# Expert results through DRAM instead of scatter products, and gate and up weights in pieces of 256 input rows

## The reference, cut to what matters

```python
def moe_swiglu(h, router, wg, wu, wd):
    logits = (h @ router).astype(jnp.float32)
    top_v, top_i = lax.top_k(logits, TOP_K)
    gates = jax.nn.softmax(top_v, axis=-1)
    out = jnp.zeros_like(h)
    for e in range(N_EXPERTS):
        gate_e = jnp.sum(jnp.where(top_i == e, gates, 0.0), axis=-1)[..., None].astype(h.dtype)
        out = out + gate_e * swiglu(h, wg[e], wu[e], wd[e])
    return out
...
x = x + moe_swiglu(rmsnorm(x, p['norm_ffn_odd'][i]), p['moe_router'][i], p['moe_w_gate'][i],
                   p['moe_w_up'][i], p['moe_w_down'][i])
y = rmsnorm(x, p['final_norm'])
```

## Time and profile before

| | us |
|---|---|
| median of 3 runs | 1320.86 (1320.65 to 1324.37) |
| the profiled execution | 1327.41 |
| its span in the profile | 1325.7 |
| TensorE busy | 1299.6 (98%) |
| VectorE busy | 373.8 (28%) |
| ScalarE busy | 169.9 (13%) |
| GpSimd busy | 61.0 (5%) |

### The profile page before, as it was taken

One profiled execution on the slowest core, in us unless ns is written; L12 is line 12 of the kernel. 1 busy time (PEld: TensorE's weight loads), 2 busy tenths in 40 slices (PEclk: granted clock), 3 DMA queues, 4 the chain that ended last, 5 costly groups with the idle time before them and its releaser, 6 DMA issues.

```text
span 1325.7 us, 17071 instructions
## 1 busy us (share of the span) xinstructions
PE 1299.6 (98%) x7217; PEld 826.4 (62%) x7217; DVE 373.8 (28%) x869; ACT 169.9 (13%) x367; POOL 61.0 (5%) x87
## 2 busy tenths in 40 slices
PE   8999999999999999999999999999999999999997
PEld 6878788888888888867843433434334444444452
DVE  5537775421111113984400110011100110110101
ACT  2241423010000100013200000000000000101002
POOL 1013110000000201100000000000000000000000
PEclk8999999999999999999799999999999999999999
DMA  8639633565456424354699999999999999899994
GB/s 289 206 130 304 221 96 96 191 179 168 127 166 223 143 72 127 132 198 197 267 388 424 408 424 425 408 424 410 424 425 424 424 406 425 323 359 418 409 423 188
DMA packets 105484, 380.81 MB, mean 287 GB/s; under 512 B 7580, under 2 KB 62796, under 8 KB 80778
## 3 DMA queue, kind: packets, MB, share of 16 engines
q1 hardware_dynamic: 97811, 359.46, 69.9%
q0 software_dynamic: 3216, 11.54, 2.7%
q10 hardware_dynamic: 4386, 8.76, 2.1%
HBM read 371.96 MB, written 8.86 MB: 287 GB/s over the span
## 4 chain that ended last, share of the span: by engine, by line
PE 89%; DVE 7%; ACT 1%; DMA 1%; SPq 1%; issue 1%; DVEq 0%; ACTq 0%
PE ps L1746 30%; PE ps L2278 21%; PE ps L2317 13%; PE ps L2264 6%; PE ps L2272 3%; DVE both L1450 3%; PE ps L1999 3%; PE ps L2328 2%; PE ps L2299 1%; PE ps L1991 1%; PE ps L1977 1%; PE ps L2211 1%; PE ps L2148 1%; PE ps L2200 1%; DMA both<-in_w_in_even_dram 1%
## 5 line engine op out<-in xcount | busy, mean ns | idle before, releaser
L1746 PE MATMUL ps<-both 128*128 128x264 f32 x2080 | 474.3, 390 | 0.5 <-DMA both<-in_w_in_even_dram 0.3
L1746 PEld LDWEIGHTS ps<-both 128*128 128x128 f32 x2080 | 397.0, 192 | 72.3 <-issue 2.7
L2278 PE MATMUL ps<-both 128*64 128x384 f32 (+1 forms) x1792 | 280.9, 466 | 0.8 <-ACT both L1050 0.8
L2278 PEld LDWEIGHTS ps<-both 128*64 128x64 f32 x1792 | 127.0, 138 | 152.6 <-issue 142.7
L2317 PE MATMUL ps<-both 128*64 128x512 f32 (+1 forms) x704 | 176.1, 596 | 0.0
L2317 PEld LDWEIGHTS ps<-both 128*64 128x64 f32 (+1 forms) x704 | 58.5, 143 | 98.6 <-issue 97.8
L1653 DVE TENSOR_TENSOR both<-both,ps 128x384 f32<-128x384 f32 (+7 forms) x46 | 20.9, 485 | 233.2 <-PE ps L2278 118.1
L2264 PE MATMUL ps<-both 128*128 128x510 f32 (+1 forms) x192 | 77.2, 559 | 0.0
L2264 PEld LDWEIGHTS ps<-both 128*128 128x128 f32 x192 | 35.9, 189 | 39.8 <-issue 32.5
L1450 DVE SCALAR_TENSOR_TENSOR both<-both,par 128x256 f32<-128x256 f32 x120 | 50.9, 481 | 1.0
L2272 PE MATMUL ps<-both 128*32 128x384 f32 (+1 forms) x512 | 47.1, 465 | 0.0
(11 more groups left out here) (369 smaller groups left out, 882.4 us busy)
## 6 DMA issues: line engine op xcount, KB each, us to landing
both<-in_moe_w_gate_dram SPq DMA_DIRECT2D x64, 1408.0 KB
both<-in_moe_w_up_dram SPq DMA_DIRECT2D x64, 1408.0 KB
both<-in_moe_w_down_dram SPq DMA_DIRECT2D x48, 1536.0 KB
both<-in_w_in_even_dram SPq DMA_DIRECT2D x10, 2048.0 KB
both<-in_moe_w_down_dram SPq DMA_DIRECT2D x16, 1024.0 KB
both<-in_ffn_w_gate_dram SPq DMA_DIRECT2D x11, 1024.0 KB
both<-in_ffn_w_up_dram SPq DMA_DIRECT2D x11, 1024.0 KB
both<-in_ffn_w_down_dram SPq DMA_DIRECT2D x4, 2816.0 KB
```

The lines of the kernel that those rows point to most:

```text
L1746: ins = mm(ps[:, 0:T], w[:, c, cols:cols + P], src[:, c, :], start=c == 0, stop=c == nk - 1)
L2278: ins = mm(ps[64 * r:64 * r + 64, 0:WIDE[k]], xg[:, c, 0:64], w[:, first:first + WIDE[k]], start=c == 0, stop=c == DC - 1)
```

## The change

**Results by DRAM.** A new DRAM table `yrows` has one row for each place in items 0 to 6 (576 rows of 4 KB, and a row that ScalarE's queue fills once from a row of `htok` which holds no token). After an item's `ysb` is filled, ScalarE's queue stores it there (2 DMAs for a 64-row item, 4 for a 96-row one, 1 for the 128-row one; semaphore `y_put`). After item 0 VectorE works out, in 14 small operations (`results_chosen`), for each token which two rows of `yrows` are its own and with which gates. When item 6 is stored, GpSimd issues three indirect fetches for the first row of each token (`fetch_results`, blocks of 128, 128 and 8 tokens), and, as each block of these has been added, three more for the second row. VectorE adds them with their gates to the residual, which is now held by token rows in `sums` (`results_added`: twice six `scalar_tensor_tensor` of 128 x 512). In VectorE's program this stands between item 6 and item 7. The products and turns for the scatter in items 1 to 7, `sum_rows` and `mark_sums` are gone. The residual is turned into token rows in items 0 to 2 (`turn_sums`, eight turns a block). Item 7 still goes back by products (`SelG`, `turn_gates` after the second up chunk), now into empty PSUM banks, and VectorE adds the six banks to `sums` before the final norm.

**Pieces of 256 rows.** Gate and up weights come in eight pieces in place of 16. Partition `p` takes input rows `2p` and `2p + 1` of its block, which lie together in DRAM: 22,528 bytes. `w_used` is still raised after each half. For item 0 the pieces are loaded as halves of 11,264 bytes a partition. The rows of `xg` follow the new order: the turns and products that make it read every second column (`in_pairs`).

The rest of the diff renames or merges semaphores. Its core:

```diff
-PIECES = 24
-RING_PIECES = 12
+PIECES = 16
+RING_PIECES = 6
...
+PAIRS = DC // 2
+UPS = PAIRS
+DOWNS = 2 * PAIRS
...
             def load_piece(of, at):
                 if at < DOWNS:
-                    c = at % DC
+                    first = 2 * P * (at % PAIRS)
                     dst = piece_cols(at)
-                    src = of[at // DC][:, P * c:P * (c + 1), :].rearrange("a p n -> p (a n)")
+                    src = of[at // PAIRS][:, first:first + 2 * P, :].rearrange("a (p i) n -> p (a i n)", i=2)
...
+            def load_half(of, at, half):
+                first = 2 * P * (at % PAIRS)
+                dst = piece_cols(at)[:, 2816 * half:2816 * (half + 1)]
+                src = of[at // PAIRS][:, first:first + 2 * P, :].rearrange("a (p i) n -> p i (a n)", i=2)[:, half]
+                sp.dma_start(dst, src).then_inc(sem(PIECE_SEMS[PIECE_SLOT[at]][0]), 16)
...
+            def fetch_results(m, k):
+                n, at = ROWS[k], 1 + BLK * m + k
+                if m:
+                    pool.wait_ge(sem("y_added"), k + 1)
+                pool.indirect_dma_start(
+                    out=yback[k][0:n, :], out_offset=None, in_=yrows[:, :],
+                    in_offset=bass.IndirectOffsetOnAxis(ap=rowidx[0:n, at:at + 1], axis=0)).then_inc(sem("y_back"), 16)
...
             for s in range(STATIC):
                 fetch_rows(s, 0)
-            pool.wait_ge(sem("ord_ready"), 2)
+            pool.wait_ge(sem("y_chosen"), 1)
+            pool.wait_ge(sem("y_put"), PUT_BASE[STATIC])
+            for m in range(2):
+                for k in range(BLK):
+                    fetch_results(m, k)
+            pool.wait_ge(sem("ord_ready"), 3)
...
+            act.dma_start(yrows[0:1, :], htok[64:65, 2, :]).then_inc(sem("hrows_stored"), 16)
...
+                if s < STATIC:
+                    act.wait_ge(sem("ysb_lo"), LO_BASE[s + 1])
+                    act.wait_ge(sem("ysb_hi"), s + 1)
+                    first = ROW_BASE[s]
+                    if cap == P:
+                        act.dma_start(yrows[first:first + P, :], ysb[:, :]).then_inc(sem("y_put"), 16)
+                    else:
+                        for h in range(2):
+                            act.dma_start(yrows[first:first + 64, 512 * h:512 * h + 512],
+                                          ysb[64 * h:64 * h + 64, 0:512]).then_inc(sem("y_put"), 16)
+                            if cap == 96:
+                                act.dma_start(yrows[first + 64:first + 96, 512 * h:512 * h + 512],
+                                              ysb[64 * h:64 * h + 32, 512:1024]).then_inc(sem("y_put"), 16)
...
+            def results_added():
+                dve.wait_ge(sem("t_free4"), USES[BLK - 1]["res"][0] + 1)
+                dve.wait_ge(sem("t_free5"), USES[BLK - 1]["res"][1] + 1)
+                n = 0
+                for m in range(2):
+                    dve.wait_ge(sem("y_back"), 48 * (m + 1))
+                    if m:
+                        dve.wait_ge(sem("y_added"), BLK)
+                        dve.wait_ge(sem("sums_added"), BLK)
+                    for k in range(BLK):
+                        rows = ROWS[k]
+                        for h in range(2):
+                            to = sums[k][h][0:rows, :]
+                            v.scalar_tensor_tensor(out=to, in0=yback[k][0:rows, 512 * h:512 * h + 512],
+                                                   scalar=gsel[0:rows, 3 * m + k:3 * m + k + 1], in1=to, op0=ALU.mult,
+                                                   op1=ALU.add).then_inc(sem("y_added" if h else "sums_added"), 1)
...
             for s in range(STATIC):
                 moe_item(s, 0)
+                if s == 0:
+                    results_chosen()
+                    dve.sem_inc(sem("banks_read"), 6)
+            results_added()
...
             with dve.Fori(0, items) as t:
                 moe_item(STATIC, t)
...
                 for c in range(DC):
                     chunk(0, c)
                     if c == 1:
-                        n5 = USES[s]["selT"][1]
-                        turn_gates(t + s, t * STEP4 + USES[s]["selT"][0], None if n5 is None else t * STEP5 + n5,
-                                   (SEQ_CAP[min(s + 1, EXP - 1)], s, t + (s + 2)))
-                    if s and 2 <= c < 2 + SCAT:
-                        scatter(SEQ_CAP[s - 1], t + s, t * STEP4 + USES[s]["selT"][0], t * STEP4 + USES[s]["scat"][0],
-                                t * STEP5 + USES[s]["scat"][1], (c - 2,))
+                        row_ids(SEQ_CAP[min(s + 1, EXP - 1)], t + (s + 2), t * STEP4 + USES[s]["ids"][0])
+                    if c == 3 and s < BLK:
+                        turn_sums(s, *USES[s]["res"])
                 for c in range(DC):
                     chunk(1, c)
                     if s == STATIC and c == 1:
...
+                        turn_gates(t + 1, t * STEP4 + USES[s]["gates"][0])
```

More of the change, by code:

```diff
@@ L85, in piece_table @@
 def piece_table():
[L87 removed]
+    cols = [2 * 2816] * DOWNS + [D * (b1 - b0) for b0, b1 in SEGS for _ in range(2)]
     at, starts = 0, []
@@ L232, in bank_uses @@
         item = {"start": tuple(at)}
[L233 to L237, removed]
+        item["ids"] = use(4)
+        if s < BLK:
+            item["res"] = use(4, 5)
+        if s >= STATIC:
+            item["gates"] = use(4)
         item["gather"] = use(4, 5)
@@ L245 @@
 STEP5 = USES[EXP]["start"][1] - USES[EXP - 1]["start"][1]
+ROW_BASE = [1 + sum(SEQ_CAP[:s]) for s in range(STATIC)]
+YROWS = 1 + sum(SEQ_CAP[:STATIC])
+PUTS = {64: 2, 96: 4, P: 1}
+PUT_BASE = [16 * sum(PUTS[SEQ_CAP[k]] for k in range(s)) for s in range(EXP)]
+LO_BASE = [sum(3 if SEQ_CAP[k] == 96 else 1 for k in range(s)) for s in range(EXP)]
 EXIT_BASE = [sum(len(EXITS[SEQ_CAP[k]]) for k in range(s)) for s in range(EXP)]
@@ L1698, in _ @@
                 moe_item(STATIC, t)
-            gates_turned(items * STEP4 + (USES[EXP]["start"][0] - STEP4))
             dve.wait_ge(sem("fgain_loaded"), 16)
@@ L2135, in _, with in_pairs @@
             keep_busy(3, accT[:, 0, :])
+            def in_pairs(rows, d):
+                return rows.rearrange("t (a p i) -> t a i p", p=P, i=2)[:, d // 2, d % 2]
             def gather(cap, value, n4, n5, halves=(0, 1)):
@@ L2158, in turn_rows_in @@
                         d = 4 * half + c
-                        out, rows = psum[4 + half][:, cap * c:cap * (c + 1)], xrow[0:cap, P * d:P * (d + 1)]
+                        out, rows = psum[4 + half][:, cap * c:cap * (c + 1)], in_pairs(xrow[0:cap, :], d)
                         if looped:
@@ L2215, in sum_rows @@
-            def sum_rows(k, h):
-                n = ROWS[k]
-                for j in range(4):
-                    mm(psum[LAST_BANK[k][h]][0:n, P * j:P * (j + 1)], accT[:, 4 * h + j, P * k:P * k + n], ident[:, :],
-                       start=j == 0, stop=False)
-            def mark_sums(opened):
-                for b, n in ((0, P), (1, P), (2, P), (3, P), (7, TS)):
-                    mm(psum[b][0:n, 0:1], ones[0:1, 0:n], ones[0:1, 0:1], start=opened, stop=not opened)
+                pe.wait_ge(sem("sel_ready"), chosen)
@@ new lines, in row_ids, with turn_gates @@
+                for b in range(BLK):
+                    ins = mm(psum[4][0:cap, BLK * P:BLK * P + 1], Sel[:, b, 0:cap], tokid[:, b:b + 1], start=b == 0,
+                             stop=b == BLK - 1)
+                ins.then_inc(sem("t_full4"), 1)
+            def turn_gates(value, n4):
+                pe.wait_ge(sem("t_free4"), n4)
+                pe.wait_ge(sem("selg_ready"), value)
+                for b in range(BLK):
+                    ins = tr(psum[4][:, P * b:P * (b + 1)], SelG[:, b, :], ident[:, :])
+                ins.then_inc(sem("t_full4"), 1)
@@ L2227, in moe_item, with turn_sums @@
+            def turn_sums(k, n4, n5):
+                n = ROWS[k]
+                for h, count in enumerate((n4, n5)):
+                    pe.wait_ge(sem(f"t_free{4 + h}"), count)
+                    for j in range(4):
+                        ins = tr(psum[4 + h][0:n, P * j:P * (j + 1)], accT[:, 4 * h + j, P * k:P * k + n], ident[:, :])
+                    ins.then_inc(sem(f"t_full{4 + h}"), 1)
             def moe_item(s, t):
@@ L2301, in turn_act, with down @@
                     ins.then_inc(sem("t_act"), 1)
-                def down(k, between=None):
+                def down(k):
                     b0, b1 = SEGS[k]
```

327 lines of the change are left out of this document (156 added, 171 removed).

## The result

The changed kernel takes **1350.95 us** (median of 4 runs, 1349.24 to 1356.43); the kernel before, beside it, 1320.96 (4 runs). The ratio is **1.0228, with a 95% interval of 1.0194 to 1.0262**: 2.3% slower, 30 us. Predicted were 1348. The profiled execution took 1356.43 us, 5.5 over the median, with a span of 1354.7.

What follows compares the result with a forecast made beforehand. TensorE was taken to set the pace, the weight stream close behind. Item 6's end 1231 + chain 65 + rest 37.5 + clock 3 = 1336.5; tail 16.5 gives span 1353, +27, so 1348 us, range 1320 to 1358.

Steps and rivals of the forecast that it cites:

- The chain in the open: Item 7: TensorE stands some 30 us awaiting VectorE's selections after item 6's store and two fetch rounds; chance 0.55, 1338 to 1358.
- The length of a turn: DMA engines after item 6: each small packet waits for one 22,528-byte weight packet, 0.85 + 0.16 = 1.01 us.
- The stores: After item 6: copy and issue 1.7 us, eight turns 7.5, landing about 1.0; result stored at T0 + 10.
- T0: The end of item 6, forecast to move from 1238.8 to about 1231 us (1227 to 1235).
- The rounds, 23 us each: Before item 7's selections: two serial rounds of three fetches, each 6 us fixed plus 17 turns (17.2 us).
- the hole: Weight stream at 1128 to 1193 us: SP's queue fills only 86.9% with the ring full; worth 8.8 us at most.
- I take nothing: Turns with strided `in_pairs` reads: free or under 1.5 us an item, taken as zero because TensorE's gain covers them.
- Net 33.5 us less work: TensorE: 37.3 us of scatter work removed less 3.8 added, of which 21.7 lie ahead of item 7.
- 11.3 us more on a stream that has no room: DMA stream: `ysb` stores add 5.8 us and fetches 5.5, with no room except in the hole.
- the second case: Rival: turns stay at 0.59 us, the chain stays hidden and the stream decides; 1328 us, chance 0.25 (1325 to 1333).
- The chain decides above T0 + 47: Item 7: selections ready later than T0 + 47 make the chain, not the stream, set the time.
- The faster case: Rival: stream closes the hole, stores go in free, packets give 4.2 us; 1314 us, chance 0.12.

Runs made afterwards that it cites:

- e7_early_round: Changed kernel with second-choice fetches issued once item 5 is stored and added first, first choices after item 6 as before; 1331.46 us, ratio 1.0081.
- e5_small_pieces: Changed kernel with weight pieces of 128 inputs again, and the loads, slots and turns of the kernel before; results still by DRAM; 1333.4 us, ratio 1.0094.
- e8_small_early_first: Changed kernel with 128-input weight pieces, second choices fetched after item 5's store, and item 7's selections ahead of the first choices' additions; 1326.82 us, ratio 1.0041.
- e4_pieces_only: Kernel before, scatter products kept, with only the pieces of 256 rows and their strided turns added; 1326.35 us, ratio 1.0034.
- e1_half_packets: Changed kernel with each gate and up piece loaded as two transfers of 11,264 bytes a partition, ring and waits unchanged; 1338.84 us, ratio 1.0128.
- e9_small_no_transfers: Changed kernel with 128-input weight pieces and without result stores, fetches and additions, scatter products still gone; 1316.11 us, ratio 0.9961.

## Why the prediction came out right, step by step

- **"The chain in the open" (0.55)** is what happened: 28.7 us of TensorE idle after the tenth chunk against "some 30", six fetches, VectorE released by their landings. The cause is shown, not argued: without the second round (`e7_early_round`) 19.5 us come back, with the selections ahead of the adds 11.8.
- **The length of a turn**, "1.01 us": measured 16.6 / 16.5 = 1.01. The forecast had no row of a large packet beside a small one; it was the one-for-one rule of the earlier trace rows and a packet's time by its bytes. With packets halved it is 0.62 (0.59 predicted for that size). The Trainium skill's rule that an engine drains a group of some 9 to 17 descriptors before it switches (DMA: Bandwidth & Descriptors, section Queues, rings and completion order) is not what these rounds show. Equal counts alone, 270 beside 264 or the earlier trace rows, would also fit groups of equal size; the order in time does not. The rate in 40 slices of 0.4 us of the first round,

```profile
GB/s 385 676 104 770 227 419 637 39 824 163 563 464 232 740 84 770 227 607 281 192 760 173 627 410 262 740 74 780 227 390 637 39 824 163 454 572 326 508 247 647
```

rises and falls about once in 1 us, a turn; groups of eight rows and eight weight packets would take an engine some 8 us. (The 0.54 us a packet that the prediction read in the earlier trace rows counts ten completion packets among the 78; the sum doesn't use it.)
- **The stores, "T0 + 10"**: measured T0 + 14.8, the term most off. From the issue at 1233.8 us to 1237.4 the queues show no packet of the store; with 1.7 us for copy and issue I had the first at T0 + 1.7, and it came at T0 + 4.4. The eight turns were right: in 1237.4 to 1245.2 us all 128 packets of data went beside 136 of weights, 7.8 us against 7.5:

```profile
DMA packets 300, 3.33 MB, mean 426 GB/s; under 512 B 36, under 2 KB 36, under 8 KB 164
```

  Then 2.6 us passed to the landing, in place of the 1.0 that I gave.
- **The rounds, 23 us each**: measured 22.4 (1248.7 to 1271.1) and 19.5 (1272.9 to 1292.4); the second ran beside smaller weight packets (306 with 4.56 MB in 1276.5 to 1290 us, where the first had 310 with 6.08), as down pieces have 12,288 bytes a partition, so its turns were shorter. I had taken all packets of the bulk for large ones. The adds took 4.05 in place of 4.5. So an error of +5 in the stores and -4 in the second round met at T0 + 66, against "T0 + 65"; that they cancel is luck. TensorE came to its wait at T0 + 37.5 (1299.1 - 28.7 - 1233.0), against "about T0 + 35".
- **T0, "1231 (1227 to 1235)"**: 1233.0 in the profiled execution, 1226.6 to 1230.3 in the other full kernels with large pieces. Right, but for a reason that I had only half: I took the hole to be capacity that TensorE's shorter work and the stores would use. With large pieces it grew, to 76.5%. "Filled" was true only with small pieces (DMA share 0.96 in `e5_small_pieces` and `e8_small_early_first`).
- **"The gain lies between 0 and 4.2 us; I take 3"** for the packets: right for the stream (last section), but a kernel that TensorE paces gets nothing of it, and `e4_pieces_only` was 4.6 us slower. The step that failed is the strided reads of `in_pairs`, "I take nothing", at most "1.5 us": the turns took 2.6 us longer, and nothing covered them there. "Up to 3.4 us once" for the first large piece is what `e1_half_packets` shows (4.92 us of waiting in place of 1.55); the 2.2 us that the clock took behind that wait were left out.
- **"Net 33.5 us less work"** on TensorE: its busy time fell by 23.3. (The prediction's parts, 13.4, 3.0 and 4.8, also add up to 21.2, not to its 21.7, and 33 packets of 0.16 us are 5.3, not 5.5.) T0 came out within 2 us even so, and behind it the chain set the time.
- **"11.3 us more on a stream that has no room"**: 10.7 by `e9_small_no_transfers` and `e8_small_early_first`. That was the best-sized term, and with it the second case could be judged: all the chain hidden gives 1326.8 with small pieces, 1331.7 with large ones, against 1328.
- **"The chain decides above T0 + 47"** was too late a threshold. In `e7_early_round` the selections were ready at T0 + 43 (1270.9 - 1227.9) and TensorE waited 3.0; in `e5_small_pieces` and `e1_half_packets` at T0 + 50, and it waited 19.1 and 11.5, with 1333.4 and 1338.8 us in the end. The case "turns stay at 0.59" is nearly `e1_half_packets`, with turns of 0.62: 1338.8, not 1328.
- **The rest and the clock**, "37.5 + 3": from 1299.1 to 1338.7, 39.5 us. **The tail**, "16.5": 16.0. The faster case (0.12) needed the hole closed and the chain below T0 + 47; even without any transfers the large pieces allow only 1322.8.

In sum: 1351 against 1348, the mechanism right, the terms' errors (+5 stores, -4 second round, +2 T0) nearly cancelling; the closeness of the number is in part luck. The spread of the runs' profiled time about the median, 5.5 us, is as large as all of them.

## What to carry to other kernels

As these runs show it, a small transfer beside a saturated queue waits for one packet of that queue at each of its own, so packet size of the bulk stream is the latency of everything else: before making bulk packets larger, count the small packets that stand on a chain in series, and look whether a round of them can be asked for earlier. A product that is swapped for bytes must be paid in the currency of the resource that is short; here TensorE gave back 5 us and the bytes took 11. And a larger piece costs at the places where the reader has caught up: it waits for all of the first piece, 4.9 us in place of 1.6 here. Look also at what a new layout does to the small operations that follow it; turns of rows with every second column took 10.1 us in place of 7.5.

## What the runs showed of the hardware that I had not expected

- TensorE's clock fell to the 1.2 GHz level around waits of only 4.9 us, and for a moment behind one of 3.1 (a mean of 0.69 in 1263.8 to 1267.2 us). In the changed kernel the granted clock is 0.50 in these windows, of which the first two begin in an item's wait for its first gate piece (TensorE went on at 884.34 and 1052.26, after 4.86 us each), and the third is the stall:

```profile
882.80:889.60 6.80, 5.26 (x20) 2.15 (x24) 0.00 (x0) 0.00 (x0) 0.00 (x0) 0.50 1.01 433
1050.10:1056.90 6.80, 4.64 (x6) 2.19 (x7) 0.00 (x0) 0.00 (x0) 0.00 (x0) 0.50 1.04 443
1275.40:1302.60 27.20, 3.46 (x13) 1.52 (x15) 6.22 (x14) 0.00 (x0) 1.80 (x3) 0.50 1.00 414
```

- The stretch ahead of item 0, at 0.50 in the earlier trace rows, ran at 1.00 in the changed kernel, and item 0's first chunk began at 652.4 us in place of 658.1. In 645 to 655 us the granted clock was 0.96 to 1.00 in the profiled executions of all ten kernels without scatter products, and 0.50 and 0.54 in the two with them. I had priced nothing of this, and didn't test what causes it. It may belong to the execution and not to the kernel: the profiled one of before had a mean granted clock of 0.987 over its span and was 6.5 us over the median, and the 41 executions of before beside the experiments had 0.990 to 0.997.

```profile
646.00:663.00 17.00, 16.22 (x120) 11.14 (x120) 9.02 (x53) 1.88 (x3) 0.98 (x1) 1.00 0.83 320
```

- Between the issue of item 6's store and its first packet lay some 3.7 us beside a full queue, with large bulk packets as with small ones: the queues show no packet of it in 1233.8 to 1237.4 us of the changed kernel, in 1226.0 to 1229.8 of `e5_small_pieces` and in 1231.0 to 1234.7 of `e1_half_packets`.
- Weight loads of TensorE that read every second float32 took 213 ns in place of 138 (64 rows; `e4_pieces_only` and before).
- Packets of 22,528 bytes moved a little more through a full queue. In 658 to 1100 us, before and then `e4_pieces_only`:

```profile
q1 hardware_dynamic: 18068, 181.08, 98.7%
```
```profile
q1 hardware_dynamic: 12423, 182.28, 98.6%
```

  0.7% more, 2.9 us at 0.42 MB/us, between the 0.4% and the 1.1% of the prediction, which took 3 us for a somewhat longer stretch.
